# Gated feed-forward loop: where VectorE computes its modulation pieces

## What is computed

```python
def ada_modulation(c, ada_w, ada_b):          # ada_w: 1024 x 6144, one per layer
    m = jax.nn.silu(c) @ ada_w + ada_b
    return jnp.split(m, 6, axis=-1)           # sh_m, sc_m, g_m, sh_f, sc_f, g_f

def swiglu(h, w_gate, w_up, w_down):          # 1024 -> 2816 -> 1024
    return (jax.nn.silu(h @ w_gate) * (h @ w_up)) @ w_down

hf = modulate(rms_norm(x, ffn_norm), sh_f, sc_f)
return x + g_f[:, None, :] * swiglu(hf, ffn_w_gate, ffn_w_up, ffn_w_down)
```

## Time and profile before

| | |
|---|---|
| median of 3 runs | 1174.51 us (1173.94 to 1174.69) |
| profiled execution, its own time | 1177.91 us |
| its span, first to last instruction | 1176.3 us |
| TensorE busy | 99% of the span |
| VectorE busy | 75% |
| ScalarE busy | 54% |
| mean granted TensorE clock | 1.000 |

### The profile page before, as it was taken

How to read it: one execution, slowest core, us unless ns; L and a number is a source line. 1 busy time by engine, 2 the same in 40 slices (tenths; PEclk the granted TensorE clock), 3 DMA queues, 4 the chain that set the end, 5 groups by cost and what they waited for, 6 DMA issues and landing times.

```text
span 1176.3 us, 22917 instructions
## 1 busy us (share of the span) xinstructions
PE 1161.4 (99%) x9553; PEld 1124.4 (96%) x9553; DVE 882.2 (75%) x1177; ACT 633.7 (54%) x853; POOL 98.4 (8%) x147
## 2 busy tenths in 40 slices
PE   8999999999999999999999999999999999999998
PEld 8999999999998999999999999999988779999998
DVE  5876778878766778778889887887777657866543
ACT  6657566633447576633558554343556665543432
POOL 0000001110034001011100001111000000000000
PEclk9999999999999999999999999999999999999999
DMA  8452568887662577787653658868846505576362
GB/s 312 156 179 72 180 220 281 303 309 247 233 233 73 180 252 256 278 317 282 234 181 129 192 159 298 277 233 297 274 147 246 181 5 188 184 262 212 120 198 84
DMA packets 150060, 248.96 MB, mean 212 GB/s; under 512 B 5554, under 2 KB 80923, under 8 KB 149979
## 3 DMA queue, kind: packets, MB, share of 16 engines
q1 hardware_dynamic: 135858, 197.17, 49.8%
q0 software_dynamic: 13952, 50.60, 11.7%
q10 hardware_dynamic: 168, 0.04, 0.0%
HBM read 246.74 MB, written 1.05 MB: 211 GB/s over the span
## 4 chain that ended last, share of the span: by engine, by line
PE 85%; DVE 5%; issue 1%; ACT 1%; DMA 1%; POOL 0%; DVEq 0%; POOLq 0%
PE ps L2153 25%; PE ps L2155 25%; PE ps L2154 25%; DVE w_lo L1262 3%; PE ps L2439 2%; DVE scratch L1764 1%; PE ps L2305 1%; PE ps L2755 1%; ACT w_hi L747 1%; PE ps L2421 1%; DMA ada_raw<-in_l_ada_w 1%; PE ps L2729 1%; PE ps L2408 1%; PE ps L2771 1%; PE ps L2238 0%
## 5 line engine op out<-in xcount | busy, mean ns | idle before, releaser
L1262 DVE TENSOR_TENSOR w_lo<-raw,w_hi 128x2048 fp32r<-128x2048 f32 (+4 forms) x196 | 412.9, 2145 | 94.3 <-ACT w_hi L747 94.0
L747 ACT ACTIVATE w_hi<-raw 128x2048 fp32r<-128x2048 f32 (+4 forms) x196 | 342.1, 1791 | 159.4 <-PE ps L2155 148.8
L2153 PE MATMUL ps<-h_both,w_hi 128*128 128x256 f32 (+1 forms) x1296 | 361.6, 279 | 2.8 <-DVE w_lo L1262 2.1
L2155 PE MATMUL ps<-h_both,w_lo 128*128 128x256 f32 (+1 forms) x1296 | 359.7, 278 | 0.0
L2154 PE MATMUL ps<-h_both,w_hi 128*128 128x256 f32 (+1 forms) x1296 | 359.7, 278 | 0.0
L2153 PEld LDWEIGHTS ps<-h_both,w_hi 128*128 128x128 f32 (+1 forms) x1296 | 242.8, 187 | 4.2 <-issue 3.4
L2155 PEld LDWEIGHTS ps<-h_both,w_lo 128*128 128x128 f32 (+1 forms) x1296 | 244.0, 188 | 0.0
L2154 PEld LDWEIGHTS ps<-h_both,w_hi 128*128 128x128 f32 (+1 forms) x1296 | 242.9, 187 | 0.1
L2153 PE MATMUL ps<-a_both,w_hi 128*128 128x256 f32 x864 | 239.1, 277 | 0.0
L2155 PE MATMUL ps<-a_both,w_lo 128*128 128x256 f32 x864 | 238.6, 276 | 0.0
L2154 PE MATMUL ps<-a_both,w_hi 128*128 128x256 f32 x864 | 238.6, 276 | 0.0
(11 more groups left out here) (425 smaller groups left out, 1814.6 us busy)
## 6 DMA issues: line engine op xcount, KB each, us to landing
ada_raw<-in_l_ada_w POOLq DMA_DIRECT2D x96, 512.0 KB, 7.0
raw<-in_mlp_w_up SPq DMA_DIRECT2D x32, 1024.0 KB, 6.6
raw<-in_mlp_w_down SPq DMA_DIRECT2D x32, 1024.0 KB, 6.4
raw<-in_l_ffn_w_gate SPq DMA_DIRECT2D x22, 1024.0 KB, 5.5
raw<-in_l_ffn_w_up SPq DMA_DIRECT2D x22, 1024.0 KB, 9.2
raw<-in_l_ffn_w_down SPq DMA_DIRECT2D x16, 768.0 KB, 5.7
raw<-in_l_w_qkv SPq DMA_DIRECT2D x12, 1024.0 KB, 6.7
raw<-in_l_w_in SPq DMA_DIRECT2D x10, 1024.0 KB, 6.3
```

Source lines behind the costliest of these rows:

```text
L747: nc.scalar.activation(w_hi[:, s.slot, cut], raw[:, s.slot, cut], ACT.Copy).then_inc(split_hi, 1)
L1262: nc.vector.tensor_tensor(w_lo[:, s.slot, cut], raw[:, s.slot, cut], w_hi[:, s.slot, cut].bitcast(F32), ALU.subtract).then_inc(split_lo, 1)
L2153: nc.tensor.matmul(to, sh, mh, start=first, stop=False, skip_group_check=True)
L2155: return nc.tensor.matmul(to, sl, mh, start=False, stop=last, skip_group_check=True)
```

## The change

In `hidden(j)` the two units of a layer 0 slot no longer stand ahead of the product. Half a unit (one instruction) is issued between the product and `a_lo`, half between `a_lo` and `split(j + 2)`, and one whole unit behind the split. In layer 1 the one unit of a slot is issued as two halves in the same two places. The number of units, their order, and the down slots' code stay as they are. A group's transpose and reduction follow its last half wherever that stands.

```diff
--- before.py
+++ after.py
@@ -1751,28 +1751,31 @@
 
             ada_sum = scratch[:, 2:4, :].rearrange("p c t -> p (c t)")
 
-            def ada_unit(m):
+            def ada_half(m, q):
 
                 slot, quarter = m % 2, m % 4
                 dve.wait_ge(ada_loaded[slot], 16 * (m // 2 + 1))
-                for q in range(2):
-                    w, c = ada_raw[:, slot, q, :], silu_c[:, 2 * quarter + q:2 * quarter + q + 1]
-                    if quarter == 0 and q == 0:
-                        ins = nc.vector.tensor_scalar(ada_sum, w, c, None, ALU.mult)
-                    else:
-                        dve.wait_ge(ada_step, m * 2 + q)
-                        ins = nc.vector.scalar_tensor_tensor(ada_sum, w, c, ada_sum, ALU.mult, ALU.add)
-                    ins.then_inc(ada_step, 1)
-
-            ada_begun = [0]
+                w, c = ada_raw[:, slot, q, :], silu_c[:, 2 * quarter + q:2 * quarter + q + 1]
+                if quarter == 0 and q == 0:
+                    ins = nc.vector.tensor_scalar(ada_sum, w, c, None, ALU.mult)
+                else:
+                    dve.wait_ge(ada_step, m * 2 + q)
+                    ins = nc.vector.scalar_tensor_tensor(ada_sum, w, c, ada_sum, ALU.mult, ALU.add)
+                ins.then_inc(ada_step, 1)
+
+            halves_begun = [0]
+
+            def ada_halves(n):
+
+                for at in range(halves_begun[0], halves_begun[0] + n):
+                    ada_half(at // 2, at % 2)
+                    if at % 8 == 7:
+                        ada_group_done(at // 8)
+                halves_begun[0] += n
 
             def ada_units(n):
 
-                for m in range(ada_begun[0], ada_begun[0] + n):
-                    ada_unit(m)
-                    if m % 4 == 3:
-                        ada_group_done(m // 4)
-                ada_begun[0] += n
+                ada_halves(2 * n)
 
             def ada_group_done(g):
 
@@ -2021,15 +2024,18 @@
                     s, ahead = Slot(f"gate_up{l}", j), Slot(f"gate_up{l}", j + 2)
                     at_pair = slice(2 * j, 2 * j + 2)
                     full = a_full[:, at_pair, :]
-                    if j < 10 or l == 0:
-                        ada_units(2 - l)
+                    halves = 1 if j < 10 or l == 0 else 0
                     dve.wait_ge(parts_done, s.before + 2)
                     dve.wait_ge(acc_out[0], turn(f"gate_up{l}", j) + 1)
                     nc.vector.tensor_tensor(full, full, two(1), ALU.mult).then_inc(acc_out[1], 1)
+                    ada_halves(halves)
                     dve.wait_ge(hid_hi, HIDDEN_BEFORE[f"ffn{l}"] + j + 1)
                     nc.vector.tensor_tensor(a_lo[:, at_pair, :], full, a_hi[:, at_pair, :].bitcast(F32),
                                             ALU.subtract).then_inc(hid_lo, 1)
+                    ada_halves(halves)
                     split(ahead)
+                    if l == 0:
+                        ada_units(1)
 
                 def add(i, blocks=(0, 1)):
 
```

## The result

The changed kernel took 1186.29 us in the median of six runs (1182.66 to 1188.31), the kernel before 1175.15 us beside it (1173.94 to 1178.78): ratio 1.008, 95% interval 1.0056 to 1.0104. It is slower, and by more than the prediction's range (to 1181.5) allows. Its profiled execution took 1184.94 us, with a span of 1183.3, against 1177.91 and 1176.3 before. So the two traces are 7.0 us apart and the two medians 11.1. Both numbers have to be explained, and neither turns out to be the cost of the change.

What follows compares the result with a forecast made beforehand. VectorE was taken to bound nine layer 0 slots, by some 0.4 us a slot. The terms -2.8 + 5.6 + 2.3 = +5.1 us on a median of 1174.5 gave 1179.6 us, range 1173.5 to 1181.5.

Steps and rivals of the forecast that it cites:

- The loop: Layer 0 gated slots: two halves go into VectorE's two waits for ScalarE, all three TensorE waits go, -2.8 us.
- The unit behind the split in the loop: Layer 0 loop: the whole unit behind the split costs nothing, the low part being done 3 us before TensorE wants it.
- The stop: Layer 0, down slot 2: unit 79's late load holds up the split, TensorE stands still for 5.6 us, +5.6 us.
- The slow restart: Behind the stop at down slot 2: TensorE's matmuls restart at a slow pace, +2.3 us.
- Layer 1: Layer 1 loop: the unit moves from VectorE's idle time into the two waits, 0 us; at most 1.4 us.
- the difference is carried over: Whole kernel: the runs' median lies 3.4 us below the profiled execution, and is assumed to after the change, giving 1179.6 us.
- The pace: Rival, either layer's loop: matmul pace changes, 3.8 us; layer 1 faster 1175.8, layer 0 slower 1183; chance 0.06 each.
- early loads: Rival, down slot 2: unit 79's load lands within 3.8 us, kernel at 1174 or a little less; chance 0.08.
- the gain alone: Rival, split of down slot 2: units behind the loop do not hold it, 1171.7 us; chance 0.10.
- the stop without a slow restart: Rival, behind the stop at down slot 2: TensorE goes on at full pace, 1177.3 us; chance 0.26.

Runs made afterwards that it cites:

- layer1_only: The kernel before with the change in layer 1 alone, layer 0 as before; median 1176.47 us, ratio 1.0013.
- after: First trace of the changed kernel, no further edit; profiled execution 1184.94 us, median of its six runs 1186.29 us.
- after_again: The changed kernel run again without an edit; median 1185.78 us of 12 executions, ratio 1.0056 to the kernel before.
- warm_stop: The changed kernel with 26 small matmuls of constants on TensorE in the stop; median 1183.91 us, ratio 1.0042.
- after_third: The changed kernel a third time without an edit; median 1184.41 us of 6 executions, ratio 1.0081 to the kernel before.
- after_fourth: The changed kernel a fourth time without an edit; median 1180.68 us of 12 executions, ratio 1.0016 to the kernel before.
- late_units: The changed kernel, layer 0's first down pair reordered: split of down slot 2, unit 78, add(0), unit 79, split of down slot 3; 1173.47 us, ratio 0.9997.
- slot10_only: The kernel before with the new order in slot 10 of layer 0 alone; median 1189.72 us, ratio 1.0079.
- before_again: The kernel before run again without an edit; median 1175.04 us of 12 executions, ratio 0.9995.
- split_first: The changed kernel with the split of down slot 2 ahead of units 78 and 79 in layer 0's first down pair; 1182.44 us, ratio 1.0049.
- before: First trace of the kernel before the change; profiled execution 1177.91 us, median of its runs beside the changed kernel 1175.15 us.

## Why the prediction was wrong

**The direction and the mechanism were right.** Every step up to the sum was found in the trace at the place and nearly the time given.

1. *The loop.* Forecast -2.8; the traces in the short pace give 98.45 against 101.30, -2.85. What the step missed: VectorE's cycle of 11.3 us hid TensorE's long pace (96 x 0.1177 = 11.3 us a slot). Where the stretch is in the long pace, little of the gain is left: by the 0.25 us of layer1_only at each of three places some 0.8 us, an estimate, since no trace has the kernel before in that pace throughout.
2. *The unit behind the split in the loop.* Forecast 0, measured 0: no wait of TensorE is left there.
3. *The stop.* Forecast a start of down slot 2 at 810.9 and a stop of 5.6 us; it came at 811.04, and the idle time is 6.3 us (5.7 to 6.3 in the four traces). The terms: landing 6.8 us for the assumed 6.6; the stages before ran 0.5 us earlier, which moves both ends; and the releaser is add(0), which ends its first half 0.4 us after the low part. I had named add(0) as queued behind the late unit, and taken the low part to be what TensorE waits for.
4. *The slow restart.* Forecast +2.3 from the start of the span; 2.0 in after and after_again, shown by warm_stop to be the clock, and 2.7 in after_third, where matmuls are 0.21 us apart for 5.7 us behind the stop and not for 4.3. (In after_fourth "rest" is 3.8 us too long, since the down slots also ran in the long pace.) The granted clock of 1.0 at the span's start, which the prediction weighed against the step, was no reading: the trace's records of the clock begin at 9.4 us, when the slow start is about over. Behind the stop the clock reads 0.50.
5. *Layer 1.* Forecast 0; no TensorE wait there.

Sum of the steps: +5.1 forecast, +5.45 between the two traces in this stretch, +6.1 in the mean of 36 against 105 executions (standard error 0.7, or 1.6 by the four sittings).

**The step that failed is the last one**, "the difference is carried over", together with the rival "The pace". The prediction saw the two paces, and gave them a chance of 0.12 for two loops, 2.6 to 4.3 us each, as if a kernel had its pace; it also took 0.2% (2.3 us) for what a measurement can tell. The traces show them to differ from execution to execution of one kernel, the two MLPs among the stages, where the long one costs 7.7 us. The four numbers that stood for the kernel before, three runs within 0.75 us and a profiled one 3.4 us above them, could have said so: the profiled trace has the long pace from 118 to 163 us and in all 864 matmuls of layer 1's loop, 1.7 + 3.8 us. The measured median of 1186.29 is a sample of six out of executions whose mean is 1183.5; the comparison 1175.15 is one from executions whose mean is 1177.4. Of the 11.8 us from 1174.5 to 1186.29, 6.1 are thus the difference of the means, and 2.9 and 2.8 us are the distances of the two medians from these means. That the first six of each fell so far apart is put down to chance, not shown. The forecast's 1179.6 starts from a median of the lower heap and could hold for fast executions alone (the ten fastest of the changed kernel lie at 1177.6 to 1181.0); chosen after the result, they confirm nothing.

Of the rivals, early loads and the gain alone did not occur (the load took 6.8 us, and the shortest of its kind in any trace, 3.9, would still not have been under the 3.8 of the prediction); the stop without a slow restart was only had by adding work (warm_stop).

## What to carry to other kernels

Moving work later within a loop moves it into what follows the loop: look at the last pass, and at every buffer that the moved work frees for a load, before counting the gain of the others. Where units share two buffers, the load of the third of three in a row starts only when the first is through, and what is queued behind the third in program order pays for the landing (6.8 us here), whether it needs the data or not; taking the queue apart at that place (late_units) kept the gain. And before a difference of 0.5% is read from medians, look at the heaps that the executions fall into, and compare one stretch between two fixed instructions in several traces.

## What the runs showed of the hardware that was not expected

- TensorE has two paces at the same granted clock of 1.00: a 256-column matmul starts every 0.113 or every 0.1177 us, 885 or 851 of them in 100 us. Most changes of pace stand where TensorE stopped for a moment or turned to other work (slot10_only at 754.82, before_again at 776.7, layer1_only at 732.0), but not all: near the start of gated slot 3 the long pace gives way to the short one with no two starts over 0.126 us apart (late_units at 703.3, slot10_only at 709.5, layer1_only at 709.2). What decides it stays open; the same program has it differently from execution to execution.
- Executions of one kernel differ by up to 15 us (1172.1 to 1187.5), in two heaps whose means, 1174.3 and 1181.5, are 7.3 us apart. Between the twelve traces, outside the stretch, the pace accounts for all but 1.9 us of a difference of up to 9.5; for executions without a trace it is not shown.
- Behind a stop of 2.9 us the granted clock was 0.50 for 3.4 us (split_first, from 0.4 us behind the restart); stops of up to 0.9 us left it at 1.00 (before, slot10_only). Filling the stop with 26 small matmuls of constants kept the clock at 1.00 (warm_stop), and gave back the 2.0 us.
